# Attention scores of a head's two maps given to the matmul engine in alternating blocks of 512 keys, both masks last

## The reference

```
sc = einsum('bhcqd,bhckd->bhcqk', q[lo:hi], k[:hi]) * scale     # both maps
sc = where(kpos <= qpos, sc, -inf)                             # causal mask
p  = softmax(sc, axis=-1)
w  = p[:, :, 0] - lam * p[:, :, 1]
out = einsum('bhqk,bhkv->bqhv', w, v[:hi])
```

## Time and profile before

| | |
|---|---|
| median of 3 runs | 3504.1 us (3502.11 to 3508.59) |
| profiled execution | 3491.37 us, span 3489.6 us |
| PE, weight loads, DVE, ACT, POOL busy | 83%, 41%, 54%, 17%, 42% of the span |
| mean granted TensorE clock | 0.904 of full speed |
| score matmuls in the trace (L884) | 192, of 64 rows |
| mask matmuls in the trace (L887) | 128, of 128 rows |

### The profile page before, as it was taken

How to read it: one execution, slowest core, us unless ns; L and a number is a source line. 1 busy time by engine, 2 the same in 40 slices (tenths; PEclk the granted TensorE clock), 3 DMA queues, 4 the chain that set the end, 5 groups by cost and what they waited for, 6 DMA issues and landing times.

```text
span 3489.6 us, 32143 instructions
## 1 busy us (share of the span) xinstructions
PE 2902.4 (83%) x10195; PEld 1420.3 (41%) x10195; DVE 1885.4 (54%) x4610; ACT 604.6 (17%) x1334; POOL 1482.7 (42%) x1348
## 2 busy tenths in 40 slices
PE   8999989886245786656669999989999899998997
PEld 3455455444112443433334444434444344443333
DVE  2334433777569666758864656645555544443113
ACT  1321133222002666820000000100000000000000
POOL 0010011233534344144456666655666566664441
PEclk9999969877567898878889999999999999999998
DMA  2100021344587899699889999999999999998993
GB/s 102 49 25 25 25 77 64 133 163 139 201 309 269 310 367 346 236 368 342 335 326 406 388 405 400 396 353 394 400 404 383 361 407 392 406 388 330 349 358 122
DMA packets 307574, 981.53 MB, mean 281 GB/s; under 512 B 29904, under 2 KB 57680, under 8 KB 306640
## 3 DMA queue, kind: packets, MB, share of 16 engines
q0 software_dynamic: 184320, 671.17, 50.8%
q1 hardware_dynamic: 120464, 307.85, 23.2%
q10 hardware_dynamic: 2624, 0.46, 0.1%
HBM read 941.63 MB, written 37.75 MB: 281 GB/s over the span
## 4 chain that ended last, share of the span: by engine, by line
PE 26%; DMA 20%; DVE 12%; POOL 7%; issue 4%; ACT 2%; DVEq 1%; ACTq 0%; SPq 0%; another core or an unknown queue 0%
DMA v_ring<-in_peer_v_dram,ids_t 14%; PE part L1694 8%; PE acc L1727 6%; PE hid L1675 6%; DMA u_ring<-in_peer_u_dram,ids_u 4%; DVE u_ring L1977 4%; POOL v_ring L1629 4%; POOL u_ring L1620 3%; PE turn_ps L1667 3%; PE part L1703 1%; ACT dense_sums L1766 1%; DMA wq_pair<-in_peer_wq_dram 1%; DVE scratch_later L1215 1%; DVE scratch_later L1213 1%; DVE idx_later L1162 1%
## 5 line engine op out<-in xcount | busy, mean ns | idle before, releaser
L1977 DVE CUSTOM_DVE_ANT_0 u_ring<-u_ring,x_rows_in 128x1024 f32<-128x1024 f32 x560 | 676.6, 1225 | 524.7 <-DMA u_ring<-in_peer_u_dram,ids_u 463.3
L1629 POOL DMA_INDIRECT v_ring<-in_peer_v_dram,ids_t x640 | 676.0, 1056 | 623.4 <-PE acc L1727 447.6
L1620 POOL DMA_INDIRECT u_ring<-in_peer_u_dram,ids_u x560 | 621.8, 1110 | 541.9 <-DVE dots L1977 337.4
L1694 PE MATMUL part<-room 128*128 128x512 f32 x1536 | 690.0, 599 | 93.2 <-DVE room L1957 84.1
L1675 PE MATMUL hid<-x1t_dense,room 128*128 128x384 f32 x2048 | 701.5, 496 | 6.6 <-DMA room<-in_peer_ut_dram 4.3
L1675 PEld LDWEIGHTS hid<-x1t_dense,room 128*128 128x128 f32 x2048 | 385.6, 193 | 346.1 <-issue 107.9
L1694 PEld LDWEIGHTS part<-room 128*128 128x128 f32 x1536 | 291.3, 192 | 451.5 <-issue 336.0
L1727 PE MATMUL acc<-v_ring,line 128*32 128x512 f32 x2560 | 347.2, 664 | 147.9 <-DMA v_ring<-in_peer_v_dram,ids_t 137.4
L1804 ACT ACTIVATE room<-hid 128x384 f32<-128x384 f32 x128 | 62.7, 490 | 1540.9 <-PE hid L1675 1277.0
L1967 DVE TENSOR_TENSOR dense_sums<-dense_sums,part 128x512 f32<-128x512 f32 x186 | 125.4, 684 | 273.3 <-PE part L1694 231.0
L414 PE MATMUL bank<-w_ring,xt 128*128 128x512 f32 x512 | 225.1, 592 | 2.6 <-issue 2.6
(11 more groups left out here) (312 smaller groups left out, 2664.5 us busy)
## 6 DMA issues: line engine op xcount, KB each, us to landing
wq_pair<-in_peer_wq_dram SPq DMA_DIRECT2D x32, 2048.0 KB
room<-in_peer_ut_dram SPq DMA_DIRECT2D x128, 512.0 KB
room<-in_peer_v_dram SPq DMA_DIRECT2D x128, 512.0 KB
gate_grid<-room SPq DMA_DIRECT2D x6, 4096.0 KB, 15.1
room<-gate_grid SPq DMA_DIRECT2D x32, 768.0 KB
w_ring<-in_w_in_dram SPq DMA_DIRECT2D x5, 2048.0 KB, 8.0
v_ring<-in_peer_v_dram,ids_t POOLq DMA_INDIRECT x640
u_ring<-in_peer_u_dram,ids_u POOLq DMA_INDIRECT x560
```

The costliest lines, as they stand in the source:

```text
L1620: pool.indirect_dma_start(u_ring[:, n % U_RING, :], None, peer_u, bass.IndirectOffsetOnAxis(ap=ids_u[:, q, k:k + 1], axis=0))\
L1629: pool.indirect_dma_start(v_ring[:, n % V_RING, :], None, peer_v, bass.IndirectOffsetOnAxis(ap=ids_t[:, q % 2, token:token + 1], axis=0))\
L1694: last = mm.matmul(part[k % 3][:], weights[:, n % 2, i, d * P:(d + 1) * P], vd[:, slot, half * 512:(half + 1) * 512], start=(i == 0), stop ...
L1977: vec.tensor_tensor_reduce(u_ring[:, n % U_RING, :], u_ring[:, n % U_RING, :], x1[:, q % 2, :], 1.0, 0.0, ALU.mult, ALU.add, dots[:, q % 2 ...
```

## The change

In `scores(n)` both `sc_free` waits come first. The blocks of 512 keys are the outer loop and the maps the inner one, so a block of map 0 is followed by the same block of map 1. Both masks stand behind all blocks; each gives its map's `sc_done`. Matmuls, operands and destinations are the same ones as before, in another order; `stop` is set on the blocks that no mask follows.

```diff
                     for c in range(2):
-                        rows = slice(c * DA_DIM, (c + 1) * DA_DIM)
                         pe.wait_ge(sc_free[c], 1).then_inc(sc_free[c], -1)
-                        for k0 in range(0, keys, 512):
-                            k1 = min(keys, k0 + 512)
-                            diagonal = k1 == keys
-                            last = mm.matmul(SC[c][:, k0:k1], q_t[rows, h, t * P:(t + 1) * P], k_t[rows, h, k0:k1],
-                                             start=True, stop=not diagonal)
-                            if diagonal:
-                                last = mm.matmul(SC[c][:, k1 - P:k1], ident[:], mask_qk[:], start=False, stop=True)
-                        last.then_inc(sc_done[c], 1)
+                    for k0 in range(0, keys, 512):
+                        k1 = min(keys, k0 + 512)
+                        for c in range(2):
+                            rows = slice(c * DA_DIM, (c + 1) * DA_DIM)
+                            mm.matmul(SC[c][:, k0:k1], q_t[rows, h, t * P:(t + 1) * P], k_t[rows, h, k0:k1],
+                                      start=True, stop=k1 < keys)
+                    for c in range(2):
+                        mm.matmul(SC[c][:, keys - P:keys], ident[:], mask_qk[:], start=False, stop=True).then_inc(sc_done[c], 1)
```

## The result

| | before | after |
|---|---|---|
| median | 3503.11 us (6 runs, 3496.70 to 3511.88) | 3478.76 us (6 runs, 3467.34 to 3485.15) |
| span of the profiled execution | 3489.6 us | 3480.2 us |
| attention block, first score matmul to barrier | 518.7 us | 498.2 us |
| PE busy in it | 384.2 us | 321.3 us |

The ratio of after to before is 0.9926, with a 95% interval of 0.9904 to 0.9948. Forecast: 3480.

A forecast was written before the change was run, and what follows sets the result against it. No single engine bounds the attention block: PE-bound or mostly so early, DVE from 624 us. Gains of 3.6, 10.6, 3.8 and 5.9 sum to 23.9 us off the 3504.1 median: 3480 us, range 3465 to 3500.

The forecast's parts named there:

- items 0 to 9: First ten of 32 attention items: a loop over both exponentials, 3.1 / 3.9 / 4.7 us, limits the gain to 3.6 us.
- burst steps 10, 14, 15, 18, 19, 22: Steps filled by output or query projection bursts (L954, L920): PE is the bound, full saving, 10.6 us.
- steps 13, 16, 17, 20: PE waits behind ACT's transposed copies after map 1's exponential: 1.8, 0.65, 0.65 and 0.7 us gained, 3.8 in all.
- steps 26, 30: Half-rate steps, 896 and 1024 keys: DVE's 3.15 us of idle limits the gain to about 2.95 and 3.0, together 5.9.
- all others: Steps 11, 12, 21, 23 to 25, 27 to 29, 31 and the tail hang on POOL or DVE: no gain.
- Overlap of the row parts: Score blocks of both maps run side by side in the array's row halves; saves PE B + 0.6 or B + 0.4.
- The lower bound (none) and its rival: Score blocks: row parts do not overlap, only 0.6 or 0.4 us of shape changes saved; 3505 us, chance 0.15.
- The clock: Attention block, loosest term: full clock could bring up to another 12 us, cold bursts and steps could cost 13.
- signs of being wrong: Map 1's blocks a full B later, clock of 528 to 624 under 1.00, or next stage growing as the block shrinks.
- the slower rival: Steps 13 to 22 fall to half clock as PE idles: +33, net +9, 3513 us; chance 0.05.
- PE busy: In the attention block, PE busy time was to fall by some 35 us.
- The barrier: End of the attention block: was to stand near 934 us, from 957.8 before.

The follow-up runs named there:

- the run without masks: Kernel before with the causal masks left out and its waits where they were, one execution: attention block 488.9 us.
- the run with two halves: Changed kernel, but items of up to 512 keys take the halves of a map's PSUM region in turn: 3465.48 us, ratio 0.9907; again 0.9916.

## Why the prediction was right, step by step

The sign and the mechanism came out, and the total too (3478.76 against 3480). That the total came out to 1.3 us is in part luck. The forecast gain was 23.9 us; in the first pair of profiles the changed kernel was 18.7 us ahead by the start of step 31, and its third profile was only 14.6 ahead of the same first profile of the kernel before. The parts, in us gained up to step 31:

| part | forecast | first profile of after | third |
|---|---|---|---|
| items 0 to 9 | 3.6 | 2.1 | 2.7 |
| burst steps 10, 14, 15, 18, 19, 22 | 10.6 | 9.4 | 8.2 |
| steps 13, 16, 17, 20 | 3.8 | 1.4 | 1.5 |
| steps 26, 30 | 5.9 | 5.1 | 2.1 |
| all others | 0 | 0.7 | 0.0 |
| sum | 23.9 | 18.7 | 14.6 |

- **Overlap of the row parts**: full, as taken. 1.15 us at half rate and 1.28 at full rate for both maps, where one map took 1.15 and 1.27. The lower bound (none) and its rival are out by the trace of after and by the run without masks.
- **Loop, items 0 to 9**: the form was right, and three runs bear it out; its constant was 0.25 to 0.3 us too small (3.39 and 4.16 against 3.1 and 3.9). In item 5 the minima are where the sum had them (2.09 us behind the scores, 0.66 apart). The handovers are not: from the second minimum's end to the exponential 0.25 us, and from its end to the next scores 0.27, where the sum had 0.15 each.
- **Burst steps**: 10, 14, 15, 18 and 19 gave 1.9, 1.2, 1.2, 1.5 and 1.5 in the first pair, each within 0.1. Step 22 gave 2.15 instead of 3.1. The step that failed is the sentence that PE is the bound there and only DVE's reading of the burst stands behind it. The first half also takes `pair_for_pe`, which ended 2.3 us before the burst in the old trace:

```profile
638.01 0.60 ACT L1026 ACTIVATE sc_pair<-bank 128x512 f32<-128x512 f32 x1 [6.68 <-ACTq L1025]
...
640.96 7.07 PE L954 MATMUL bank<-w_ring,mix_t 128*128 128x512 f32 x16
```

  PE's work ahead of the burst became 4.4 us shorter: the 3.1 of the scores, and 1.2 because full clock came back at 625.3, during the transposes behind them (in the old trace at 641.0). Only 2.2 of it could be used; 2.19 us of wait took the rest. In all three profiles of the changed kernel this burst starts 8.24 us behind the step's start, whatever PE does.
- **Steps 13, 16, 17, 20**: 13 gave 1.75. At full clock, as in the run with two halves, 16, 17 and 20 took 6.87, 6.87 and 7.46: 0.6, 0.6 and 0.7 less, the 0.65 of the prediction. In the changed kernel half clock fell on 560.4 to 563.8 and on 604.8 to 608.2; 16 and 20 gave 0.2 and 0.0, and 17 lost 0.6.
- **Steps 26 and 30**: the first half of the burst waited 2.75 and 1.51 us for `pair_for_pe`, which the prediction did not name. In step 30 DVE's ratio then held the second half, as forecast. In step 26 it did not:

```profile
700.08 8.80 PE L953 MATMUL bank<-w_ring,mix_t 128*128 128x512 f32 x16 [2.75 <-PEq L949]
...
707.08 1.15 DVE L1057 SCALAR_TENSOR_TENSOR probs<-probs,ratio 128x896 f32<-128x896 f32 x1
...
709.03 0.69 DVE L1079 SCALAR_TENSOR_TENSOR x<-x,bank 128x512 f32<-128x512 f32 x1 [0.80 <-DVEq L1078]
```

  Half clock made the first half 8.80 us long instead of 7.1, and DVE waited 0.80 us for it. In the third profile that half took 7.10 and DVE's ratio did hold the second one, which then lost time to half clock itself. So both steps gained only 1.1 and 1.0 us there, and step 22, whose first half met half clock, 0.5.
- **The clock.** The rise that could have brought 12 us did not come in the first pair: items 0 to 9 stayed at half clock, with PE busy 32 of 43.5 us. In the third profile their mean was 0.58, and they took 42.8 us. Of the signs of being wrong, the clock under 1.00 did show: 0.96 from 526.3 to 615.0, the items of the old 528 to 624. It cost some 2.3 us in steps 16, 17 and 20 (7.27, 8.07 and 8.16 us against the 6.87, 6.87 and 7.46 above), far from the 33 of the slower rival. That 33 is a slip as well: its terms as written (14, 3.1 and about 8) add up to 25.
- **PE busy**: forecast to fall by some 35 us, it fell by 63. The slip is in the forecast's own arithmetic: B + 0.6 or B + 0.4 for each of 32 items, at the clock of the old trace, is 60. It decided nothing: 42 of these 63 us turned into idle time of PE.
- **The barrier** stood at 939.15, not near 934; 1.8 us of that lie ahead of the block. Of the block's 20.5 us, 1.8 lie behind the start of step 31, where the same changed kernel took 148.6, 152.6 and 151.9 us, and the kernel before 150.4 twice.

The medians differ by 24.4 us. The kernel before reached step 31 after 368.3 us in one profile and after 375.2 in the next, so the lead of the changed kernel there is anything from 14.6 to 25.5 us, by the pair of profiles that is taken. What the single terms lacked in the first pair, 0.8 to 2.4 us each, is smaller than this spread; what each step did is shown, how much of the median's gain each term gave is not.

## What to carry to other kernels

Matmuls that fill 64 rows ran side by side here when they lay in different row halves of the array and had no full-array matmul between them (they wrote different banks; the same bank was not tried). Look for a mask, a transpose or a bias matmul that separates them. Before you group such work, ask which wait now stands ahead of all of it: here it closed a loop over two exponentials, which alone cost 7 us, and a second buffer, free for half of the items, opened it. Where a saving has no visible wait to fall into, go through every semaphore ahead of the next long instruction and note how early each was given, since one that never showed as a wait can be the next bound: here 2.3 us of slack ahead of the burst capped what 4.4 us less work could give.

## What the hardware showed that was not expected

- Row halves of the array didn't start their matmuls in the order of the program: with whole maps one behind the other, four passes of map 0 ahead of four of map 1, the passes started in pairs 0.01 us apart, and the mask followed after 1.28 us.
- The same kernel was granted different clocks from one execution to the next in the same steps: full from 528.4 us on in one profile of the kernel before, half until 544.1 in the other, which is worth up to 4.4 us in one step.
